# Gathered expert rows in blocks of eight with a lag of ten, in place of blocks of four with a lag of six

## The reference, cut to what matters

```
s1 = einsum('thd,nd->thn', q[:, :, 0], k1);  s2 = einsum('thd,nd->thn', q[:, :, 1], k2)
v1, i1 = top_k(s1, 16);  v2, i2 = top_k(s2, 16)
score, ci = top_k(all sums v1 + v2, 16)
expert = i1[ci // 16] * 128 + i2[ci % 16]
g = softmax(score)
act = gelu(einsum('thkd,td->thk', u_tab[expert], t))
out = einsum('thk,thkd->td', g * act, v_tab[expert])
```

## Time and profile before

| | |
|---|---|
| median of 3 runs | 4214.59 us (4211.92 to 4215.84) |
| the profiled execution | 4214.59 us, of which its span is 4212.8 us |
| PE busy / DVE busy / ACT busy / POOL busy | 84% / 52% / 22% / 24% of the span |
| first dot of the 384 rows / last dot ends | 3177.2 us / 4186.6 us |
| last matmul ends / span ends | 4199.9 us / 4212.8 us |
| gathers at L2802 | 384, of 1 MB each |

### The profile page before, as it was taken

The page is one execution under the profiler, slowest core; times in us unless marked ns, Lnnn a source line. Parts: engine busy times, 40 slices in busy tenths (PEclk is TensorE's granted clock), DMA queues, the critical chain, the costliest instruction groups (busy, mean ns, idle before and its releaser), DMA issues.

```text
span 4212.8 us, 32784 instructions
## 1 busy us (share of the span) xinstructions
PE 3524.5 (84%) x10814; PEld 1824.8 (43%) x10814; DVE 2178.2 (52%) x4912; ACT 913.3 (22%) x1974; POOL 1028.2 (24%) x953
## 2 busy tenths in 40 slices
PE   8368999999998999979999985568996776777877
PEld 4244544444444564546644564224442332333332
DVE  0557324431004466756516438864138888756555
ACT  1224402000023123632211212111122222211111
POOL 0214400000000003700000004344354433444442
PEclk9767999999999999979899998779998998898998
DMA  3010021343221212210122346766689998999997
GB/s 147 18 50 1 9 98 69 135 160 127 92 80 45 84 62 68 93 60 36 60 95 78 114 165 219 271 223 231 204 310 398 382 377 343 378 421 421 417 421 304
DMA packets 116615, 765.12 MB, mean 182 GB/s; under 512 B 13112, under 2 KB 13112, under 8 KB 55776
## 3 DMA queue, kind: packets, MB, share of 16 engines
q0 software_dynamic: 102608, 580.04, 35.8%
q1 hardware_dynamic: 13824, 182.97, 11.6%
q10 hardware_dynamic: 16, 0.02, 0.0%
HBM read 744.08 MB, written 18.89 MB: 181 GB/s over the span
## 4 chain that ended last, share of the span: by engine, by line
PE 53%; DVE 17%; DMA 10%; issue 4%; ACT 3%; POOL 2%; DVEq 0%; POOLq 0%; ACTq 0%
PE ps L252 14%; PE ps L258 12%; DMA arena<-in_uv,arena 10%; DVE arena L2832 7%; PE ps L1416 6%; PE ps L2739 6%; PE ps L1346 5%; PE ps L1722 2%; PE ps L220 2%; POOL arena L2802 1%; PE ps L1709 1%; DVE arena L2642 1%; DVE arena L2648 1%; DVE arena L2644 1%; PE ps L786 1%
## 5 line engine op out<-in xcount | busy, mean ns | idle before, releaser
L2739 PE MATMUL ps<-arena 128*128 128x512 f32 x2048 | 1010.9, 650 | 332.8 <-ACT arena L2757 313.5
L2739 PEld LDWEIGHTS ps<-arena 128*128 128x128 f32 x2048 | 411.9, 207 | 910.6 <-issue 856.2
L252 PE MATMUL ps<-arena 128*128 128x512 f32 (+1 forms) x1768 | 760.3, 591 | 32.6 <-ACT arena L2271 24.2
L2832 DVE CUSTOM_DVE_ANT_0 arena<-arena 128x1024 f32<-128x1024 f32 x512 | 623.1, 1219 | 238.2 <-DMA arena<-in_uv,arena 238.0
L2802 POOL DMA_INDIRECT arena<-in_uv,arena x384 | 439.6, 1145 | 557.0 <-PE ps L2739 334.2
L258 PE MATMUL ps<-arena 128*128 128x512 f32 (+2 forms) x1408 | 530.2, 537 | 3.1 <-DVE arena L1263 0.9
L252 PEld LDWEIGHTS ps<-arena 128*128 128x128 f32 x1768 | 339.4, 193 | 439.4 <-issue 435.2
L258 PEld LDWEIGHTS ps<-arena 128*128 128x128 f32 x1408 | 267.5, 191 | 262.4 <-issue 217.9
L220 PE MATMUL ps<-arena 128*128 128x128 f32 x1046 | 196.4, 324 | 202.9 <-ACT arena L812 49.5
L2799 POOL DMA_INDIRECT arena<-in_uv,arena x256 | 263.7, 1030 | 386.0 <-PE ps L2739 143.3
L1416 PE MATMUL ps<-arena 128*128 128x512 f32 x640 | 293.9, 606 | 20.1 <-ACT arena L1802 12.8
(11 more groups left out here) (343 smaller groups left out, 3453.2 us busy)
## 6 DMA issues: line engine op xcount, KB each, us to landing
arena<-in_w_in SPq DMA_DIRECT2D x27, 2048.0 KB, 8.8
arena<-in_w_ada SPq DMA_DIRECT2D x12, 2048.0 KB, 8.2
arena<-in_w_ff_in SPq DMA_DIRECT2D x8, 2048.0 KB, 12.5
arena<-in_w_ff_out SPq DMA_DIRECT2D x8, 2048.0 KB, 12.7
arena<-in_w_pq SPq DMA_DIRECT2D x8, 2048.0 KB, 8.5
aside<-arena POOLq DMA_DIRECT2D x20, 512.0 KB, 5.6
arena<-in_uv,arena POOLq DMA_INDIRECT x640, 8.6
arena<-in_w_at SPq DMA_DIRECT2D x4, 2048.0 KB, 8.4
```

What stands on the lines that cost most here:

```text
L252: x = t.matmul(PS[:, b, 0:n], hT[:, k, i * 128:(i + 1) * 128], w[:, k, :], start=k == 0, stop=k == nk - 1)
L2739: x = t.matmul(PS[:, b + c, :], DG[n % 4], row(f)[:, 512 * c:512 * c + 512], start=j == 0, stop=j == 127)
L2832: v.tensor_tensor_reduce(row(f), row(f), TT[i], 1.0, 0.0, ALU.mult, ALU.add, DOT[i % 2][:, j:j + 1]).then_inc(*pe.V.step("dot", 128 * i + j))
```

## The change

Two constants of the list. For token tiles 1 to 3 a block has 8 rows and not 4, and `pv` of a row stands 10 entries behind its `pu` and not 6.

```diff
-        BLOCK = (16, 4, 4, 4)
-        LAG = 6
+        BLOCK = (16, 8, 8, 8)
+        LAG = 10
```

## The result

The changed kernel takes 4356.9 us (median of 4 runs, 4349.8 to 4365.9) against 4213.3 us beside it on the same chip: a ratio of 1.034, 95% interval 1.032 to 1.036. The forecast was 4290.4 us with a range up to 4325. It is slower, as forecast, but by 144 us and not by 76.

The account below looks back on a forecast made before the run. DVE was taken to bound the first stretch, DMA the second, PE the end. First stretch +8, second +53.7, normalization +5 and end +9.1 sum to +75.8 on 4214.6, giving 4290.4 us; 8-in-10 range 4250 to 4325.

Parts of the forecast that it names:

- What bounds the kernel: DVE sets the pace up to 3627.1 us, DMA up to 4186.6; then only PE's last rows and a normalization.
- Buffers held longer is the term that decides: At a block's last dot eleven of 14 buffers are taken, not seven, leaving three gathers under way instead of seven.
- When the first gather lands: Behind a block's last landing L, the next gather lands at L + 11.94 us, 2.0 us late, with PE starting slow.
- the other seven gathers are on time. A block of eight costs 19.9 + 2.0 = 21.9 us: Second stretch, DMA-paced: only one gather per block is late; 28 blocks take 613.2 us against 559.5, +53.7.
- The first stretch: Part with selection, up to 3627.1 us: late gathers eat the saved chains; +8 us, bounds -16 and +24.
- The normalization: In the second stretch, POOL's gather held behind it lands late: +5 us, bounds 0 and +8.
- The end: Last dot to last matmul: eleven rows on PE instead of seven, +9.1 us, or +6.9 at full clock.
- PE keeps its clock: Rival: PE's bunches start at full clock, gathers only 0.2 us late; 4228 us, chance 0.08.
- More than one late gather a block: Rival: slower landing or a late second buffer piles up late gathers in both stretches; 4329 us, chance 0.12.

Follow-up runs that it names:

- pure-DMA runs: Kernel before, but for token tiles 1 to 3 V half left out, buffer free after its dot; two, three or four gather buffers: 4615, 4352 and 4225 us.
- b8_l7: Changed kernel with lag 7 in place of 10, blocks of eight kept: 4209.7 us, ratio 0.9994 to the kernel before.
- warm: Changed kernel with 14 filler matmuls on PE behind each bunch of eight rows from row 176 on: 4345.7 us, ratio 1.031 to the kernel before.
- b4_l10: Changed kernel with blocks of four in place of eight, lag 10 kept: 4401.0 us, ratio 1.045 to the kernel before.
- b4_l6_m10: Kernel before (blocks of four, lag 6) with ten gather buffers in place of 14: 4410.9 us, ratio 1.047.
- b8_l7_m11: Changed kernel with lag 7 in place of 10 and eleven gather buffers in place of 14: 4373.1 us, ratio 1.038 to the kernel before.
- b8_l9: Changed kernel with lag 9 in place of 10, blocks of eight kept: 4270.0 us, ratio 1.014 to the kernel before.

## Why the prediction was right in kind and wrong in size

- *What bounds the kernel* held: DVE in the first stretch, DMA in the second, PE behind the last dot.
- *Buffers held longer is the term that decides* held, and is shown. Lag alone (1.045), buffers alone (1.047) and the whole change (1.034) are slow; the block alone is not (0.999).
- *When the first gather lands* held in the block shown, 10.64 us after the last dot against 10.69.
- **The step that failed** is "the other seven gathers are on time. A block of eight costs 19.9 + 2.0 = 21.9 us". The rule behind it was that DMA is at full pace as soon as any gather is behind the one that lands. The pure-DMA runs show 2.9 to 3.0 us a row with two under way. In the changed kernel the second, third and fourth gather behind a block end cost 0.4, 0.75 and 0.15 us more than 2.49, though POOL issued them when I had expected. The stretch measured 663.6 us and not 613.2 + 5, so 45 us of the miss are here: 28 blocks of 23.2 and not 21.9 us are 36 of them.
- *The first stretch* was +23.9 and not +8, 16 us of the miss, at the very edge of its bounds. The same gathers are late there: DVE waits 42.0 us for them. b8_l7 shows the saving that is hidden beneath it: -11 us, where I had allowed up to 16.
- *The normalization* was not told apart by a run, but the traces show it. The 16 intervals up to the dot of row 271 add up to 54.9 us, 8.6 more than two average blocks; before they added up to 40.9, 1.1 over 16 x 2.49. That is 7.5 us more and not 5, within the bounds. *The end* was mis-sized by half a microsecond: +8.6 for +9.1, with DVE waiting 21.1 us for PE where I had 21.5. Together, 45 + 16 - 0.5 - 2.6 for the earlier start are 58 us, the 134 of the two spans less the 76 forecast; the other 8 us are the profiled execution's distance from the median.
- *PE keeps its clock*, the first rival, would have put the time at 4228 us. With the clock mostly kept it was 4345.7. The clock did fall as forecast (PE idles 6.5 and 8.6 us ahead of the two bunches that the trace shows around 3800), but I had given it 1.8 of the 2.0 us a block, and most of that is lost without it as well: blocks with a full-clock bunch in warm took their first late row no sooner.
- *More than one late gather a block*, the third rival with a chance of 0.12, was right in kind, at 4329 us still too small, and not by its causes: the first gather took 5.7 us on average and not 6.3, and the second was issued 2.3 us behind it, on time. Against it I had written that it does not pile up from block to block. That is true, and it was no argument: it adds up within each block. The rule of the Trainium skill, TensorE: Matmul & The Clock Gate, "HAM oscillation — how this bites in real kernels", that every bunch after a long wait starts slow, agrees with this trace: 15.8 and 16.6 us for the eight rows after idle times of 8.6 and 6.5 us, where a bunch at full clock took 14.0 in warm. It did not decide the time.

The rows for the right size were in the trace before. I had looked only at how long a gather takes when nothing is ahead of it, and that held. Between 3510 and 3620 us, where POOL had been held up, nine gathers had one other under way at the end of their issue; they took 5.5 to 8.6 us to land, with a median of 6.7. Three of them, issued at 3524.00, 3567.58 and 3590.79, took

```profile
arena<-in_uv,arena POOLq DMA_INDIRECT x1, 7.1
arena<-in_uv,arena POOLq DMA_INDIRECT x1, 7.0
arena<-in_uv,arena POOLq DMA_INDIRECT x1, 7.6
```

and landed 2.9, 3.2 and 3.3 us behind the one ahead and not 2.49, though they were issued only 2.2, 1.7 and 1.8 us behind it.

## What to carry to other kernels

Before a buffer is held for longer, count what is left under way at the worst moment, here buffers - (lag + 1), and read from a place in the trace where the queue was that short how fast it moves then. The time to land in an empty queue does not give it. A lag wants to be as short as the block allows; a larger block can pay only where the engine that it relieves sets the pace. Here it won 11 us in the first stretch (b8_l7) and nothing clear of noise in the whole time.

## What the runs showed of the hardware that I had not expected

- The DMA queue needs three 1 MB gathers under way, not two, for full pace: 289, 354 to 360 and 416 GB/s with one, two and three. The buffered kernels agree. I took rows 176 to 383 of before, the changed kernel, b4_l10, b8_l7, b4_l6_m10, warm, b8_l7_m11 and b8_l9, only gathers that DVE waited for, and the start of the dot as the landing. A gather that found n others under way at the end of its issue landed behind its forerunner by 5.1 us (n = 0, 30 gathers), 3.6 (n = 1, 272), 2.8 (n = 2, 465) and 2.5 (n = 3, 277). With n = 0 and 1 a part of that is that it was issued late.
- DMA's busy share hides this: 91% busy at 355 GB/s in the changed kernel, 100% at 416 before. In the second stretch of the changed kernel one 8 KB packet in a hundred took over 0.97 us, up to 2.0, where the median is 0.31; before, one in a hundred took over 0.32. What makes them slow stays open.
- A lower clock of PE costs next to nothing where its matmuls only free buffers in time: b8_l7 runs at a granted clock of 0.87 in the second stretch, the kernel before at 0.91, and their times do not differ.
